# A decoder layer with expert gathers on one Trainium2 core: the prompt's eight tiles in five parts (1, 1, 2, 2, 2) in place of four (2, 2, 2, 2)

## The chip, the core and the metric

The kernel runs on one core of one Trainium2 chip. The metric is the device time of one launch in microseconds. The profile is of one further execution. Engines are named as in the profile: PE (TensorE matmul), PEld (its weight loads), DVE (VectorE), ACT (ScalarE), POOL (GpSimd), SP (SyncE, which issues ordinary DMAs).

## What is computed

One layer for 1024 prompt tokens (eight tiles of 128) and 8 sample tokens, with all numbers in float32:

```python
n1 = rmsnorm(x, norm1_g)
proj = n1 @ w_in                 # q/k/v, GLA q/k/v, output gate, forget gate input, two branch gates
oa = attention over a window of 128 positions, with sinks
og = gated linear attention: a recurrence over the tokens, state (4, 128, 256)
u = sigmoid(ga) * oa + sigmoid(gb) * og
h = x + u @ w_out
x' = h + peer(rmsnorm(h, norm2_g))
```

```python
def peer(...):                    # per token: 8 heads x 16 experts = 128 pairs
    q = xk @ peer_wq
    s = q . subkeys ; top 16 of each half ; top 16 of the 256 sums -> eidx
    g = softmax(sv)
    act = gelu(peer_u[eidx] . xk)             # a row of 1024 numbers for each pair
    return sum(g * act * peer_v[eidx])        # another row of 1024 numbers for each pair
```

So every tile needs 128 gathers of `u` rows and 128 of `v` rows; a gather takes one row of 4 KB for each of the 128 tokens, 512 KB together.

## The kernel before

The prompt is worked in **parts** (`c` in the code; `CH[c]` is the number of tiles in part `c`, `FIRST[c]` its first tile). A part goes through these **stages**, each for all tiles of the part together: norm; `fm` (19 blocks of the feature-major projection, L966); `va`; attention (`at`, L982 to L1007, with the `vb` units); the forget gate (`gate`, L1029); the recurrence (`gla`, L1053 to L1072, four heads); the projections `rb`, `gb` and the branch gate `ga`; the merge (`mg`) and `wo`; the second norm (`n2`); the routing query with the best keys of each half (`q`, L1123, L1130, L1631 to L1642); and `rt`, the choice of the 128 pairs on DVE (`route_tile`), which writes `eidx` at L1539. The eight sample tokens ride along in part `SC` = 2 as a ninth short tile, with stages of their own (`sgla`, `sr`).

All weights come as 38 units of 1 MB (`UNITS`) through `wring`, two buffers deep, and every part loads all 38 again (L738). A unit of `fm` or `wq` has the weights as the stationary operand and the part's tokens as the moving one, so its matmuls are 128 x (128 times the number of tiles). A token-major unit (L926) has one run of eight 128x256 matmuls for each tile.

**Gathers beside the mixer.** The experts of tile t are gathered and used while the next part is computed. The work is cut into **steps** of two pairs (`pool_quad`, `pe_quad`, `act_quad`, `dve_quad`): POOL issues two `u` rows and, 12 pairs later in the order (`LAG`), the `v` rows, through a ring of 12 rows (`ringb`, L662); DVE forms the dot products (L1428); the weighted sum of the `v` rows is formed partly on PE (with a diagonal matrix, L836) and partly on DVE (L1473). Each of the tiles has 64 steps. The first part has no tile before it and runs with no steps at all. In every later part `marks(c)` spreads the steps of the tiles of the part before evenly over the stages: at each point of the program, PE, ACT, DVE and SP first work off all steps up to the mark (`beside`, `quads`). POOL has nothing else to do and is held only by `eidx` and by free ring rows. `MARGIN` = 8 steps are left over at a part's end. `BY_PE` says what share of the `v` rows PE takes in a stage.

The tiles of a part after its first are routed late: the first tile's `eidx` is made at the end of the part, the others' inside the next part's `fm` stage.

```python
def marks(c):
    lo = 0 if c == 1 else SEG_STEP[SEG_OF[FIRST[c - 1]]] - MARGIN
    hi = SEG_STEP[SEG_OF[FIRST[c]]] - MARGIN
```

**The first part's order.** `mixer_order(c)` has two orders: for part 0, if it has two tiles, attention and recurrence are interleaved by hand and the `ga` units stand behind them (`together(c)` is then true); for all others attention comes first, then the gates, then the recurrence with a `ga` unit inside it.

```python
    if c or CH[c] != 2:
        return at + [("between", 0), ("gate", 0), ("gate", 1)] + [x for pair in zip(A, B) for x in pair]
```

**The end.** When the last part is done, its two tiles' experts are left. From `WHOLE` on (the last tile; step 394 = `QW` + 6) the `u` and the `v` row of a pair come as one piece of 8 KB from an array that holds both side by side (L657), into twelve pieces of space that the mixer no longer needs.

Of the kernel before, what the change touches and what calls it, by code (L numbers as in the profile page):

```python
# [8 lines left out]
SEQ = 1024  # L9
NS = 8  # L10
TILES = SEQ // P
CH = (2, 2, 2, 2)
NCH = len(CH)
TM = max(CH)
SC = 2
ST = TM
FIRST = [sum(CH[:c]) for c in range(NCH)]
CM = TM * P
# [35 lines left out]
DIAGS = 4  # L54
XS = FIRST[SC] + CH[SC] - 1
MARGIN = 8
# [108 lines left out]
def tiles_of(c):  # L165

    return [(t, P) for t in range(CH[c])] + ([(ST, NS)] if c == SC else [])


def pair_jobs(c):  # L170

    return [(t, min(2, CH[c] - t), P) for t in range(0, CH[c], 2)] + ([(ST, 1, NS)] if c == SC else [])

# [1873 lines left out]
```

## Time and profile before

| | before |
|---|---|
| median of 3 runs | 3768.2 us (3760.38 to 3772.49) |
| profiled execution, its own time | 3731.8 us |
| its span | 3730.0 us |
| mean granted TensorE clock | 0.871 |
| PE busy | 2881.6 us (77%) |
| DVE busy | 2804.2 us (75%) |
| POOL busy | 2234.3 us (60%) |
| ACT busy | 735.9 us (20%) |
| moved by DMA | 1294.61 MB, mean 347 GB/s |

A part ends, for this text, where the `eidx` of its first tile is written (L1539). These writes stand at 457.4, 1186.5, 2109.9 and 2987.8 us, so the parts take 458, 729, 923 and 878 us, and the end 742 us. A share of busy time is a mean over stretches with different limits; the stretches are read one by one below. In windows, a dot product is two records (the operation and a read of its accumulator), and a float32 matmul is two records as well.

### The profile page before, as it was taken

The numbers are of one execution on the slowest core, as the hardware profiler recorded it, in microseconds if no ns is written. First come the engines' busy times: TensorE is split into PE (matmuls) and PEld (weight loads), VectorE is DVE, ScalarE is ACT, GpSimd is POOL, SyncE is SP. The second block draws the span as 40 slices with busy tenths as digits, with TensorE's granted clock in tenths as the row PEclk, the third lists the DMA queues.
The fourth block names the chain that finished last, engine by engine and source line by source line (L and its number), as shares of the span: only waits on it lengthen the run. The fifth ranks groups of instructions, "written<-read, shape, count | busy, mean of one in ns | idle before, by whom it ended". The sixth has DMA issues, their size and how long they took to land.

```text
span 3730.0 us, 33134 instructions
## 1 busy us (share of the span) xinstructions
PE 2881.6 (77%) x10016; PEld 1798.5 (48%) x10016; DVE 2804.2 (75%) x5740; ACT 735.9 (20%) x1784; POOL 2234.3 (60%) x1820
## 2 busy tenths in 40 slices
PE   8888589788687999788988776978769755655665
PEld 6777566456562666453665344635556311111111
DVE  0641797887788957876879997888788867777776
ACT  1321113322111123223111111422211111111111
POOL 0000076787567656875766777778767776555553
PEclk9899799999898998888999888989879877777677
DMA  4124399999999999989999999999999998999997
GB/s 153 46 87 167 116 405 403 360 358 401 421 391 357 384 354 333 337 318 371 389 396 389 326 389 372 394 353 361 387 421 398 330 392 366 426 426 426 426 426 329
DMA packets 304256, 1294.61 MB, mean 347 GB/s; under 512 B 35288, under 2 KB 44528, under 8 KB 251184
## 3 DMA queue, kind: packets, MB, share of 16 engines
q0 software_dynamic: 260352, 1082.25, 74.2%
q1 hardware_dynamic: 43728, 210.25, 14.5%
q8 instruction: 82, 1.34, 0.1%
q14 instruction: 94, 0.77, 0.1%
HBM read 1276.77 MB, written 17.66 MB: 347 GB/s over the span
## 4 chain that ended last, share of the span: by engine, by line
DMA 26%; PE 23%; POOL 21%; DVE 16%; issue 9%; DVEq 2%; ACT 1%; PEld 1%; PEldq 0%; ACTq 0%; SPq 0%; POOLq 0%
POOL ringb L662 20%; DMA ringb<-in_v,eidx 9%; PE bank L926 8%; DMA ringb<-in_uv,eidx 7%; PE vsum L836 6%; DVE ringb L1428 4%; PE bank L1123 3%; DMA arena<-in_uv,eidx 3%; DMA n2t<-in_uv,eidx 2%; DVE acc L1473 2%; DMA wring<-in_uv,eidx 2%; PE bank L966 2%; DVE scT L1844 1%; DMA ringb<-in_u,eidx 1%; PE bank L982 1%
## 5 line engine op out<-in xcount | busy, mean ns | idle before, releaser
L662 POOL DMA_INDIRECT ringb<-in_u,eidx x768 | 920.3, 1198 | 859.5 <-DVE eidx L1539 455.3
L836 PE MATMUL vsum<-ringb,diag 128*128 128x512 f32 x1908 | 1081.8, 711 | 416.9 <-DMA ringb<-in_v,eidx 261.2
L662 POOL DMA_INDIRECT ringb<-in_v,eidx x768 | 921.6, 1200 | 327.0 <-issue 219.9
L1428 DVE CUSTOM_DVE_ANT_0 ringb<-ringb,n2t 128x1024 f32<-128x1024 f32 x776 | 922.7, 1223 | 118.0 <-DMA ringb<-in_u,eidx 56.2
L836 PEld LDWEIGHTS vsum<-ringb,diag 128*128 128x128 f32 x1908 | 399.8, 223 | 982.3 <-issue 706.1
L926 PE MATMUL bank<-wring,nTb 128*128 128x256 f32 x3024 | 686.7, 388 | 32.6 <-DMA wring<-in_w 29.0
L926 PEld LDWEIGHTS bank<-wring,nTb 128*128 128x128 f32 x3024 | 548.2, 183 | 175.0 <-DMA wring<-in_w 34.4
L1473 DVE SCALAR_TENSOR_TENSOR acc<-ringb,wgt,acc 128x1024 f32<-128x1024 f32 x354 | 454.9, 1285 | 111.7 <-DMA ringb<-in_v,eidx 107.8
L1160 ACT ACTIVATE diag<-cst,wgt 128x128 f32<-128x128 f32 x542 | 209.7, 398 | 962.4 <-DVE wgt L1445 599.3
L966 PE MATMUL bank<-nTb,wring 128*128 128x256 f32 (+1 forms) x1152 | 266.8, 390 | 6.1 <-DMA wring<-in_w 3.1
L657 POOL DMA_INDIRECT ringb<-in_uv,eidx x126 | 178.0, 1412 | 140.7 <-DVE vgb L1473 71.2
L966 PEld LDWEIGHTS bank<-nTb,wring 128*128 128x128 f32 x1152 | 225.9, 196 | 61.6 <-issue 21.3
L1123 PE MATMUL bank<-nTb,wring 128*128 128x256 f32 (+1 forms) x1024 | 234.8, 383 | 1.2 <-ACT nTb L1179 1.2
L1123 PEld LDWEIGHTS bank<-nTb,wring 128*128 128x128 f32 x1024 | 194.9, 192 | 50.2 <-issue 23.6
L1428 DVE CUSTOM_DVE_ANT_0 ringb<-ringb,oab 128x1024 f32<-128x1024 f32 x126 | 154.1, 1225 | 76.0 <-DMA ringb<-in_uv,eidx 76.0
L1179 ACT ACTIVATE arena<-bank 128x256 f32<-128x256 f32 (+1 forms) x160 | 71.5, 467 | 498.4 <-PE bank L1123 277.3
L938 PE MATMUL bank<-cst,oab 128*128 128x128 f32 (+1 forms) x216 | 40.0, 362 | 125.2 <-DVE oab L1676 60.5
L836 PE MATMUL vsum<-wring,diag 128*128 128x512 f32 x88 | 62.3, 847 | 49.9 <-ACT diag L1160 49.9
L938 PEld LDWEIGHTS bank<-cst,oab 128*128 128x128 f32 (+1 forms) x216 | 36.2, 198 | 131.5 <-DVE oab L1676 44.7
L836 PE MATMUL vsum<-nTb,diag 128*128 128x512 f32 x88 | 65.3, 884 | 44.4 <-ACT diag L1160 44.4
L836 PE MATMUL vsum<-qkb,diag 128*128 128x512 f32 x84 | 63.0, 891 | 38.3 <-ACT diag L1160 38.1
L1200 ACT ACTIVATE Pbb<-bank 128x512 f32<-128x512 f32 (+1 forms) x60 | 33.1, 552 | 292.7 <-PE bank L926 292.6
(290 smaller groups left out, 3080.1 us busy)
## 6 DMA issues: line engine op xcount, KB each, us to landing
wring<-in_w SPq DMA_DIRECT2D x152, 1024.0 KB, 7.8
ringb<-in_u,eidx POOLq DMA_INDIRECT x768, 7.3
ringb<-in_v,eidx POOLq DMA_INDIRECT x768, 7.5
n2t<-scratch_n SPq DMA_DIRECT2D x14, 512.0 KB, 7.1
oab<-in_xp SPq DMA_DIRECT2D x4, 1024.0 KB, 6.8
bTb<-in_keysT SPq DMA_DIRECT2D x4, 1024.0 KB, 11.4
vgb<-in_xp SPq DMA_DIRECT2D x4, 1024.0 KB, 8.9
arena<-in_s SPq DMA_DIRECT2D x8, 512.0 KB, 10.2
```

The source lines that it names most:

```text
L657: pool.indirect_dma_start(out=piece[s], out_offset=None, in_=a["uv"], in_offset=place).then_inc(piece_here[s], 16)
L662: pool.indirect_dma_start(out=ring[r], out_offset=None, in_=a["u"] if kind == "u" else a["v"], in_offset=place)\
L836: last = mm(out[:, g * 512:(g + 1) * 512], lhs, row[:, g * 512:(g + 1) * 512], start=(x == first), stop=(x == end))
L926: last = mm(ps[0:R, i * UC:(i + 1) * UC], nT[:, k, lo:lo + R], w[:, k, :], start=(k == 0), stop=(k == KC - 1))
L938: last = tr(ps[:, i * R:(i + 1) * R], oa[0:R, t, k * P:(k + 1) * P], ident[0:R, 0:R])
L966: last = mm(ps[0:M, 0:wide], lhs, nT[:, k, 0:wide], start=(k == 0), stop=(k == KC - 1))
L982: last = mm(ps[:, i * 256:(i + 1) * 256], qaT[lo:lo + 64, 4 * Q + 2 * g + i, t * P:(t + 1) * P], kaT[lo:lo + 64, Q, t * P:(t + 2) * P], st ...
L1123: last = mm(ps[:, 0:wide], w[:, k, (q % 2) * P:(q % 2 + 1) * P], nT[:, k, 0:wide], start=(k == 0), stop=(k == KC - 1))
L1160: A(diag[:, n % DIAGS, :], ident, ACT.Copy, scale=wgt[:, m % 2, at:at + 1]).then_inc(diag_ready, 1)
L1179: A(dst, src, ACT.Copy, scale=scale).then_inc(evac["act"].sem, evac["act"].did(key))
L1428: v.tensor_tensor_reduce(out=row, in0=row, in1=n2, scale=1.0, scalar=0.0, op0=ALU.mult, op1=ALU.add, accum_out=dg[:, m % 2, at:at + 1]).th ...
L1473: STT(y, row, wgt[:, m % 2, at:at + 1], y, ALU.mult, ALU.add).then_inc(used(("v", x))[0], 1)
```

## The change

The table of parts gets five entries. Nothing else is edited.

```diff
-CH = (2, 2, 2, 2)
+CH = (1, 1, 2, 2, 2)
```

All other tables follow from it. The parts begin at tiles 0, 1, 2, 4, 6. Part 0 and part 1 hold one tile each; part 2 (still `SC`) holds tiles 2 and 3 and the sample tokens; the last part is again tiles 6 and 7. The segments of expert work are 0, 1, 2, 3, S, 4, 5, 6, 7 where they were 0, 1, 2, 3, 4, 5, S, 6, 7. The marks of the parts with gathers now run over the steps 0 to 56 (part 1), 56 to 120 (part 2), 120 to 252 (part 3) and 252 to 386 (part 4); they ran over 0 to 120, 120 to 248 and 248 to 386. `QW` stays 388 and `WHOLE` stays 7. Part 0 no longer has two tiles, so `together(0)` is false.

The start of PE's program, before (bank is PSUM, nTb the normalized tokens, wring the weights, kaT and arena keys and queries, Pbb the scores):

```order
L938 MATMUL bank<-cst,oab 128x128 x16
L966 MATMUL bank<-nTb,wring 128x256 x144
L966 MATMUL bank<-nTb,wz 16x256 x8
L926 MATMUL bank<-wring,nTb 128x256 x16
L1029 MATMUL bank<-zbT,wg 128x256 x4
L982 MATMUL bank<-kaT,arena 128x256 x4
L926 MATMUL bank<-wring,nTb 128x256 x16
L982 MATMUL bank<-kaT,arena 128x256 x4
L995 MATMUL bank<-cst,Pbb 128x128 x8
```

and with the change:

```order
L938 MATMUL bank<-cst,oab 128x128 x8
L966 MATMUL bank<-nTb,wring 128x128 x144
L966 MATMUL bank<-nTb,wz 16x128 x8
L926 MATMUL bank<-wring,nTb 128x256 x8
L982 MATMUL bank<-kaT,arena 128x256 x4
L926 MATMUL bank<-wring,nTb 128x256 x8
L982 MATMUL bank<-kaT,arena 128x256 x4
L926 MATMUL bank<-wring,nTb 128x256 x8
L995 MATMUL bank<-cst,Pbb 128x128 x8
```

The same 144 projection matmuls have half the columns, a token-major unit has 8 matmuls in place of 16, and the gate (L1029) has moved behind the attention.

PE in part 2, from the gate to the second head of the recurrence, before (vsum is the weighted sum of `v` rows, two matmuls for each row):

```order
L1029 MATMUL bank<-zbT,wg 128x256 x4
L1034 MATMUL bank<-fmS,wg 128x8 x4
L836 MATMUL vsum<-ringb,diag 128x512 x12
L1053 MATMUL bank<-arena 128x128 x7
L1053 MATMUL bank<-qkb 128x128
L1053 MATMUL bank<-arena 128x128 x7
L1053 MATMUL bank<-qkb 128x128
L1057 MATMUL bank<-cst,arena 128x128 x2
L836 MATMUL vsum<-ringb,diag 128x512 x4
...
L836 MATMUL vsum<-ringb,diag 128x512 x6
L926 MATMUL bank<-wring,nTb 128x256 x16
L926 MATMUL bank<-wring,nTb 8x256 x8
L836 MATMUL vsum<-ringb,diag 128x512 x6
```

and with the change:

```order
L1029 MATMUL bank<-zbT,wg 128x256 x4
L1034 MATMUL bank<-fmS,wg 128x8 x4
L836 MATMUL vsum<-ringb,diag 128x512 x8
L1053 MATMUL bank<-arena 128x128 x7
L1053 MATMUL bank<-qkb 128x128
L1053 MATMUL bank<-arena 128x128 x7
L1053 MATMUL bank<-qkb 128x128
L1057 MATMUL bank<-cst,arena 128x128 x2
L836 MATMUL vsum<-ringb,diag 128x512 x4
...
L836 MATMUL vsum<-ringb,diag 128x512 x2
L926 MATMUL bank<-wring,nTb 128x256 x16
L926 MATMUL bank<-wring,nTb 8x256 x8
L836 MATMUL vsum<-ringb,diag 128x512 x2
```

The part's own matmuls are the same; about half the rows of the gathered experts stand between them.

## Rows read from the trace of the kernel before

**Rows 1.** The page: busy time of the engines over the whole span.
```profile
PE 2881.6 (77%) x10016; PEld 1798.5 (48%) x10016; DVE 2804.2 (75%) x5740; ACT 735.9 (20%) x1784; POOL 2234.3 (60%) x1820
```
**Rows 2.** The page: DMA busy tenths and GB/s in 40 equal slices.
```profile
DMA  4124399999999999989999999999999998999997
GB/s 153 46 87 167 116 405 403 360 358 401 421 391 357 384 354 333 337 318 371 389 396 389 326 389 372 394 353 361 387 421 398 330 392 366 426 426 426 426 426 329
```
**Rows 3.** Windows, one for each part and one for the end.
```profile
core 0: us, PE busy (x) PEld busy (x) DVE busy (x) ACT busy (x) POOL busy (x), PEclk, DMA share, GB/s
0.00:458.00 458.00, 369.04 (x1792) 317.70 (x1792) 192.79 (x582) 92.82 (x209) 2.17 (x13) 0.92 0.31 112
458.00:1187.00 729.00, 595.22 (x2236) 405.16 (x2236) 611.88 (x1244) 166.36 (x367) 529.21 (x446) 0.91 0.99 385
1187.00:2110.00 923.00, 805.06 (x3000) 496.69 (x3000) 728.27 (x1550) 209.25 (x508) 630.19 (x516) 0.90 0.95 360
2110.00:2988.00 878.00, 675.75 (x2372) 440.85 (x2373) 731.00 (x1457) 178.56 (x403) 650.01 (x547) 0.89 0.98 377
2988.00:3730.00 742.00, 436.50 (x618) 138.11 (x616) 540.23 (x910) 88.87 (x297) 422.76 (x301) 0.74 0.97 403
```
**Rows 4.** Waits: who held POOL before its first gather.
```profile
POOL ringb L662 <- DVE eidx L1539: 455.3, 1, 455.3
```
**Rows 5.** Windows of the dot products alone (L1428), parts 1 to 3: DVE busy.
```profile
458.00:1187.00 729.00, 277.04 (x464) 0.91 0.99 385
1187.00:2110.00 923.00, 306.83 (x516) 0.90 0.95 360
2110.00:2988.00 878.00, 327.23 (x548) 0.89 0.98 377
```
**Rows 6.** Windows of part 0: norm, fm, mixer, gates, merge, query, choice.
```profile
0.00:22.00 22.00, 3.65 (x16) 3.27 (x16) 4.46 (x9) 5.16 (x7) 2.11 (x12) 1.00 0.57 217
22.00:90.00 68.00, 67.87 (x305) 57.52 (x305) 0.03 (x1) 6.89 (x18) 0.00 (x0) 1.00 0.38 136
90.00:234.00 144.00, 117.28 (x602) 98.35 (x602) 96.43 (x198) 49.35 (x121) 0.00 (x0) 0.86 0.11 39
234.00:320.00 86.00, 83.92 (x393) 73.65 (x392) 15.52 (x28) 15.76 (x33) 0.00 (x0) 1.00 0.41 147
320.00:361.00 41.00, 33.31 (x160) 28.97 (x160) 5.49 (x8) 7.49 (x13) 0.00 (x0) 0.92 0.59 203
361.00:424.00 63.00, 62.27 (x318) 55.42 (x316) 38.74 (x224) 6.86 (x18) 0.00 (x0) 1.00 0.41 152
424.00:458.00 34.00, 0.75 (x5) 0.52 (x4) 32.11 (x116) 1.29 (x2) 0.06 (x1) 0.57 0.09 31
```
**Rows 7.** Timeline of PE in part 0: runs of 256 and of 128 columns.
```profile
22.13 64.36 PE L966 MATMUL bank<-nTb,wring 128*128 128x256 f32 x288 [0.83 <-DVE nTb L1684]
127.21 1.04 PE L995 MATMUL bank<-cst,Pbb 128*128 128x128 f32 x8
```
**Rows 8.** DMA issues: the weights at 20 to 90 us, and over the span.
```profile
wring<-in_w SPq DMA_DIRECT2D x9, 1024.0 KB, 4.7
...
wring<-in_w SPq DMA_DIRECT2D x152, 1024.0 KB, 7.8
```
**Rows 9.** Timeline of PE: two heads of part 0's recurrence begin.
```profile
197.31 1.80 PE L1053 MATMUL bank<-ringb 128*128 128x128 f32 x14 [1.00 <-issue]
...
221.66 3.33 PE L1053 MATMUL bank<-ringb 128*128 128x128 f32 x14 [8.42 <-issue]
```
**Rows 10.** Windows of part 2: attention, recurrence, sample recurrence with gates.
```profile
1339.00:1505.00 166.00, 152.71 (x686) 101.45 (x684) 117.88 (x222) 50.65 (x138) 98.58 (x85) 0.87 0.90 329
1531.00:1665.00 134.00, 115.10 (x433) 71.97 (x433) 114.34 (x183) 33.84 (x58) 98.99 (x77) 0.88 0.90 327
1665.00:1852.00 187.00, 169.29 (x603) 92.01 (x601) 142.98 (x227) 47.06 (x106) 130.80 (x101) 0.93 0.98 376
```
**Rows 11.** Window of part 2, the sums of `v` rows on PE alone (L836).
```profile
1187.00:2110.00 923.00, 304.16 (x564) 115.78 (x564) 0.90 0.95 360
```

## The prediction

> **What bounds the kernel now.** I read the page first, then the program by parts, then part 0 by stages. Over the whole span no engine is full: PE 77%, DVE 75%, POOL 60% [rows 1]. The slices show two regimes: five slices with DMA at 1 to 4 tenths, then 9 tenths to the end [rows 2]. By parts [rows 3]: part 0 has no gathers, and POOL waits 455.3 us for the first `eidx` [rows 4]; parts 1 to 3 have PE 82, 87 and 77% busy, DVE 84, 79 and 83%, DMA 99, 95 and 98%; the end has DMA at 97% and 403 GB/s.
>
> The question is which of these near-full resources sets the pace of parts 1 to 3. DMA's share says the stream of gathers. But at the same share the rate is 385, 360 and 377 GB/s there and 426 in five slices of the end [rows 2, 3]; in the attention and the recurrence of part 2 it is 329 and 327, with PE at 92 and 86% of these windows [rows 10]. There the mixer's own work, with the steps placed between, sets the pace, and the ring is merely kept full. The Trainium skill (Perfetto Trace Analysis, Identifying the Most-Contended Engine) says to judge DMA by the bandwidth of memory and not by occupancy, since 16 engines make occupancy misleading. By that rule the parts are at 85 to 90% of the 426 that this trace reaches, so not purely bound by DMA.
>
> So I treat a part beside gathers as own work plus a price for each step. The dot products give the steps: 464, 516 and 548 records are 116, 129 and 137 steps [rows 5]. A step costs PE 304.16 / 129 = 2.4 us [rows 11] and DVE 306.83 / 129 = 2.4 us for dots [rows 5] and about 1.2 us for its share of the sums. Between part 0 and part 1, both of two tiles, lie 729 - 458 = 271 us for 116 steps [rows 3]: **2.3 us a step**. The most that a step costs is a whole part over its steps, 729 / 116 = 6.3 us.
>
> **The change, part by part.**
>
> **Part 0, one tile: 458 -> 310.** By the stages of [rows 6]:
> - norm 22 -> 19: the loads stay, one tile's statistics and transposes go.
> - fm 68 -> 41. A 256-column record takes 64.36 / 288 = 223 ns; at 128 columns the eight of L995 give about 115 ns with their tail off [rows 7]. A unit is then 32 x 0.113 = 3.6 us. But a buffer of the ring is reloaded only after use, and a load lands 4.7 us after issue [rows 8]: with two buffers a unit takes (3.6 + 4.7 + 0.4)/2 = 4.35 us. Nine make 39, and 2 for the block of 16 columns. Weights, hidden today, become the pace.
> - mixer 144 -> 110. Halving gives 72, but the chains do not halve and the hand-made overlap is lost. One unit of `va` 4; six steps of attention, four of them with PE work of 2 + 3.5 + 1 + 1.9 = 8.4 us, 39; the gate with its table loads 16, now in nobody's shadow; four heads at 12.5 make 50 (with two tiles a head without much beside it takes 221.66 - 197.31 = 24.4 us [rows 9]).
> - gates 86 -> 38: eight units outside the recurrence in place of twelve, each (3.5 + 4.7 + 0.3)/2 = 4.25 us, and 4 at the ends.
> - merge 41 -> 30, query 63 -> 37 (eight units at 4.65), choice 34 -> 32 (one tile's choice already).
>
> Sum 307, called 310; ends 290 and 345. A page would put fm lower: the Trainium skill (TensorE: Matmul & The Clock Gate, Back-to-back issue gap) gives some 81 ns for a matmul of 128 columns in a stream, which would make a unit (2.6 + 4.7 + 0.4)/2 = 3.85 us and this stage 4 us shorter. The row shows about 113 ns, and the row is used.
>
> **Part 1, one tile beside tile 0: new, 425.** Its marks end at step 56; parts ended some 4 steps before their marks (116 for 120), so 52 steps. Own work 310 - 10 (the first loads) = 300; 52 x 2.3 = 120; and 5 for weights, which land in 7.8 us beside gathers [rows 8], a unit of (3.5 + 7.8)/2 = 5.7 us, mostly filled with steps. Lower end 390, which is what DMA needs: 44 MB at 2.5 us and 200 gathers at 1.4 us. (Parts 1 to 3 hold 446, 516 and 547 gathers, by POOL's counts, and 47, 62 and 44 MB besides, in 722, 877 and 860 us of busy DMA [rows 3]; these two prices fit all three within 3%.) Upper end 470.
>
> **Part 2, two tiles and the sample beside tile 1 alone: 923 -> 745.** This carries the forecast. Its own matmuls stay; 64 steps remain of 129. PE's own work is 805.06 - 304.16 = 501 us [rows 3, 11], DVE's about 270. The 65 steps removed give back a price between 2.4 us (PE's share alone, PE being 87% busy) and 6.3 (all on the path; excluded, since it would leave 514 us, just PE's own busy time with no step in it). I take 2.6, near PE's row: 923 - 169 = 754, and 10 less as only one tile comes before, with none routed late. Ends: 501 + 64 x 2.4 = 655 busy on PE, hence 670; and 825 at 1.5 a step. DMA needs only some 510 us here (256 gathers at 1.4, 62 MB at 2.5): **it idles nearly a third of this part**, and what it fails to move here it cannot move elsewhere.
>
> **Parts 3 and 4: 1607 -> 1680.** They are the old parts 1 and 3 in kind: two tiles beside two tiles. Together they hold 132 + 134 = 266 steps for 253. The 13 more at 5.6 us (2.1 MB at 377 GB/s) are 73 us. The eight loads of the samples' rows, once at the border of the end, now stand in SP's queue among the weights of part 4's fm stage, each held by the use of the row two before it: 0 to 25 us, taken at 0, since the marks pace the weights there too. Ends 1650 and 1720.
>
> **End: 742 -> 742.** It starts at the same step with the same pieces.
>
> **Sum** against the profiled execution: 310 + 425 + 745 + 1680 = 3160 where 458 + 729 + 923 + 878 = 2988 stood: **+172 us**, 3731.8 -> 3904. Its own time is 36 us under the median; on the median I forecast 3768.2 + 172 = **3940 us**. In short: 148 us less at the start buys a second pass of one tile's chains (300) and 100 us of weights (38 MB at 2.5), and a part 2 that can't use the stream.
>
> **The rivals.**
> - **Faster: the stream is the pace everywhere.** If DMA at 95 to 99% means what it says, parts 1 to 4 take the old 2530 us plus 38 MB of weights at 2.5 us, 100, and the stream starts 148 us earlier: 3768 - 148 + 100 = 3720. It decides if part 2 takes under about 570 us with part 1 at 425. For it: the shares. Against it: PE's 655 us of work in part 2 and the 327 GB/s of [rows 10]. Chance 0.08.
> - **All lower ends at once:** 295 + 390 + 670 + 1650 = 3005, +17, 3785: mixer and steps overlap nearly perfectly. Against it: a head's chain of DVE, ACT and PE in turn leaves 8.42 us idle on PE with no step beside it [rows 9]. Chance 0.09, half of it within the bound of no change.
> - **Worse: chains don't shrink.** Part 0 at 345, part 1 at 470, part 2 at 825, parts 3 and 4 at 1690: 3330, +342, 4110. For it: dependent small operations cost nearly as much for one tile as for two. Chance 0.10.
> - **The change does not do what it says:** were the last tiles' pieces or the samples' place to break the order of the end, the end would differ. `QW` and `WHOLE` are the same numbers, so I leave it 0.01, at 3990.
>
> **How the numbers follow.** The forecast has 0.72. Its own range, from half-way ends, is 3850 to 4030. For 8 in 10 it reaches to the rivals on both sides: 3835 to 4050. A difference of about 0.3% is what a measurement of this kernel can tell from none. Faster: 0.08. Same: 0.04. Slower: 0.88.
>
> **What would show it.** First `eidx` at 310 (290 to 345), with PE waiting for `wring` in fm; the second about 425 later; part 2 near 745 with DMA's share at 0.7 to 0.8 and well under 330 GB/s, PE at 85 to 90%; parts 3 and 4 at 6.3 us a step with DMA at 0.95 and more; the end at 742. The forecast is wrong if part 2 keeps DMA above 0.9, or if the first two parts together take under 600 us.

## The result and the profile after

The changed kernel is slower: 3944.39 us median (3919.72 to 3954.34, 4 runs) against 3770.34 us (3760.38 to 3775.82, 4 runs), a ratio of 1.0455 with a 95% interval of 1.0401 to 1.0509. It is +174 us on the medians. The profiled execution took 3940.9 us, with a span of 3939.1.

The profiled executions differ by 209 us, more than the medians, because the one of before lay 39 us under the median of 3770.34 and the one of after 3 us under its own. Single spans compared below carry an uncertainty of that size. So do parts: experiment 4's kernel has the same parts 1 to 3 as the kernel before, and in its profile they took 741, 940 and 897 us where [rows 3] have 729, 923 and 878, some 2% more.

The same views as of before. From the page of the changed kernel, busy time and the DMA slices (answering to [rows 1, 2]):

```profile
PE 2919.1 (74%) x10584; PEld 1843.7 (47%) x10584; DVE 2827.0 (72%) x5840; ACT 766.7 (19%) x1871; POOL 2219.2 (56%) x1820
...
DMA  5358899867677779999999999999999999999997
GB/s 193 108 191 317 325 387 390 307 240 270 209 278 263 283 253 362 381 387 345 357 408 420 356 339 415 374 375 347 351 419 393 370 327 364 426 426 426 426 426 333
```

All engines have nearly the same busy time as before in a longer span. The stream starts in the fourth slice, two slices earlier than in [rows 2], but from the eighth to the fifteenth it runs at 209 to 307 GB/s.

The windows by part, and the dot products alone (two records each, two dots a step), parts 1 to 4, answering to [rows 3, 5]:

```profile
core 0: us, PE busy (x) PEld busy (x) DVE busy (x) ACT busy (x) POOL busy (x), PEclk, DMA share, GB/s
0.00:305.00 305.00, 197.54 (x1180) 174.43 (x1180) 119.93 (x383) 64.87 (x149) 2.11 (x12) 0.89 0.44 159
305.00:729.00 424.00, 316.75 (x1380) 233.64 (x1380) 290.69 (x644) 90.87 (x214) 237.36 (x203) 0.86 0.93 355
729.00:1473.00 744.00, 645.20 (x2717) 433.22 (x2716) 477.44 (x1135) 163.97 (x412) 311.00 (x258) 0.91 0.75 262
1473.00:2322.00 849.00, 651.74 (x2319) 429.78 (x2320) 706.87 (x1422) 178.82 (x397) 622.93 (x512) 0.88 0.97 373
2322.00:3196.00 874.00, 684.33 (x2387) 435.85 (x2386) 684.62 (x1344) 181.19 (x403) 633.60 (x533) 0.89 0.97 375
3196.00:3939.00 743.00, 423.50 (x604) 136.76 (x603) 547.50 (x917) 87.01 (x296) 412.24 (x306) 0.76 0.96 400
```

```profile
305.00:729.00 424.00, 128.76 (x216) 0.86 0.93 355
729.00:1473.00 744.00, 152.46 (x256) 0.91 0.75 262
1473.00:2322.00 849.00, 310.41 (x520) 0.88 0.97 373
2322.00:3196.00 874.00, 318.60 (x532) 0.89 0.97 375
```

| part | before | steps | after | steps | forecast |
|---|---|---|---|---|---|
| 0 | 458 | 0 | 305 | 0 | 310 |
| 1, one tile | | | 424 | 54 | 425 |
| 2, with the samples | 923 | 129 | 744 | 64 | 745 |
| the two others of two tiles | 729 + 878 | 253 | 849 + 874 | 263 | 1680 |
| end | 742 | 134 | 743 | 135 | 742 |

Part 2 has PE at 645.20 / 744 = 87% and DMA at 75%. Its attention, its recurrence and its sample recurrence with gates, answering to [rows 10]:

```profile
838.00:965.00 127.00, 121.97 (x638) 88.60 (x636) 73.18 (x159) 38.34 (x117) 48.07 (x44) 0.92 0.70 242
990.00:1099.00 109.00, 91.35 (x380) 62.31 (x381) 85.71 (x139) 25.74 (x42) 47.30 (x37) 0.89 0.62 209
1099.00:1264.00 165.00, 152.03 (x571) 86.00 (x570) 93.29 (x158) 37.79 (x91) 66.69 (x52) 0.93 0.77 273
```

The three take 127, 109 and 165 us where [rows 10] have 166, 134 and 187: with half the steps they lose 12 to 23%, and the rate of DMA falls with them. The stages of part 0 (norm, fm, mixer, gates, merge, query, choice), answering to [rows 6]:

```profile
0.00:19.00 19.00, 1.94 (x8) 1.57 (x8) 2.44 (x6) 4.01 (x5) 2.11 (x12) 1.00 0.59 224
19.00:62.00 43.00, 38.52 (x304) 36.97 (x304) 0.01 (x1) 4.99 (x18) 0.00 (x0) 1.00 0.58 199
62.00:165.00 103.00, 71.15 (x361) 60.04 (x360) 55.16 (x144) 35.66 (x80) 0.00 (x0) 0.85 0.26 91
165.00:205.00 40.00, 31.87 (x143) 26.26 (x141) 7.64 (x19) 9.47 (x22) 0.00 (x0) 1.00 0.64 236
205.00:234.00 29.00, 17.68 (x80) 14.33 (x80) 3.41 (x7) 4.74 (x8) 0.00 (x0) 0.93 0.70 249
234.00:275.00 41.00, 36.39 (x288) 35.25 (x288) 22.86 (x117) 5.42 (x18) 0.00 (x0) 0.93 0.58 210
275.00:305.00 30.00, 0.00 (x0) 0.00 (x0) 28.41 (x93) 0.58 (x1) 0.00 (x0) 0.54 0.09 34
```

### The profile page after: what moved, and what is told of

Same layout as the page of the kernel before. It is cut to its first block, busy times and chain, and to the rows that moved or that the text cites. A ratio compares the mean times of both kernels' runs of the same rounds, so it can differ in the third digit from the quotient of the medians.

```text
span 3939.1 us, 34706 instructions
## 1 busy us (share of the span) xinstructions
PE 2919.1 (74%) x10584; PEld 1843.7 (47%) x10584; DVE 2827.0 (72%) x5840; ACT 766.7 (19%) x1871; POOL 2219.2 (56%) x1820
## 4 chain that ended last, share of the span: by engine, by line
PE 26%; DMA 25%; DVE 20%; POOL 14%; issue 10%; DVEq 2%; ACT 1%; another core or an unknown queue 1%; ACTq 1%; SPq 0%; PEldq 0%; PEld 0%; POOLq 0%
POOL ringb L662 13%; PE bank L926 10%; DMA ringb<-in_uv,eidx 7%; PE vsum L836 5%; DVE ringb L1428 5%; DMA ringb<-in_v,eidx 5%; DMA wring<-in_w 4%; DVE acc L1473 3%; PE bank L966 3%; DMA arena<-in_uv,eidx 3%; PE bank L1123 2%; DMA n2t<-in_uv,eidx 2%; DMA wring<-in_uv,eidx 2%; PE bank L982 1%; PE bank L1053 1%
## 5 line engine op out<-in xcount | busy, mean ns | idle before, releaser
L662 POOL DMA_INDIRECT ringb<-in_u,eidx x768 | 945.9, 1232 | 986.7 <-DVE dg L1428 479.7
L836 PE MATMUL vsum<-ringb,diag 128*128 128x512 f32 x1908 | 1083.3, 710 | 472.1 <-DMA ringb<-in_v,eidx 278.8
L662 POOL DMA_INDIRECT ringb<-in_v,eidx x768 | 897.1, 1168 | 423.6 <-issue 218.5
L1428 DVE CUSTOM_DVE_ANT_0 ringb<-ringb,n2t 128x1024 f32<-128x1024 f32 x776 | 923.7, 1223 | 148.9 <-DMA ringb<-in_u,eidx 69.1
L836 PEld LDWEIGHTS vsum<-ringb,diag 128*128 128x128 f32 x1908 | 398.7, 223 | 1021.7 <-issue 725.6
L926 PE MATMUL bank<-wring,nTb 128*128 128x256 f32 x3024 | 701.7, 391 | 62.8 <-DMA wring<-in_w 54.7
L966 PE MATMUL bank<-nTb,wring 128*128 128x128 f32 (+2 forms) x1440 | 283.4, 359 | 28.4 <-DMA wring<-in_w 25.5
L966 PEld LDWEIGHTS bank<-nTb,wring 128*128 128x128 f32 x1440 | 248.2, 208 | 79.8 <-DMA wring<-in_w 28.2
L1123 PE MATMUL bank<-nTb,wring 128*128 128x128 f32 (+2 forms) x1280 | 247.8, 349 | 11.9 <-DMA wring<-in_w 9.9
L1123 PEld LDWEIGHTS bank<-nTb,wring 128*128 128x128 f32 x1280 | 214.5, 200 | 59.8 <-issue 25.0
L1428 DVE CUSTOM_DVE_ANT_0 ringb<-ringb,oab 128x1024 f32<-128x1024 f32 x126 | 154.3, 1226 | 77.7 <-DMA ringb<-in_uv,eidx 77.7
L1179 ACT ACTIVATE arena<-bank 128x256 f32<-128x256 f32 (+2 forms) x184 | 76.0, 429 | 553.9 <-PE bank L1123 232.3
L1721 DVE SCALAR_TENSOR_TENSOR Pbb<-cst,bank 128x256 f32<-128x256 f32 x128 | 46.9, 415 | 128.7 <-PE bank L982 126.0
L1053 PE MATMUL bank<-arena 128*128 128x128 f32 x448 | 73.6, 331 | 62.8 <-DVE arena L1832 42.9
L1631 DVE MAX8 val<-bank 128x8 f32<-128x128 f32 (+1 forms) x144 | 36.7, 288 | 99.2 <-PE bank L1130 74.9
L1053 PEld LDWEIGHTS bank<-arena 128*128 128x128 f32 x448 | 69.5, 242 | 75.5 <-DVE arena L1832 51.9
```

Source lines behind the costliest of these rows:

```text
L662: pool.indirect_dma_start(out=ring[r], out_offset=None, in_=a["u"] if kind == "u" else a["v"], in_offset=place)\
L836: last = mm(out[:, g * 512:(g + 1) * 512], lhs, row[:, g * 512:(g + 1) * 512], start=(x == first), stop=(x == end))
L926: last = mm(ps[0:R, i * UC:(i + 1) * UC], nT[:, k, lo:lo + R], w[:, k, :], start=(k == 0), stop=(k == KC - 1))
L966: last = mm(ps[0:M, 0:wide], lhs, nT[:, k, 0:wide], start=(k == 0), stop=(k == KC - 1))
L1053: last = mm(ps[:, i * P:(i + 1) * P], kk, qq, start=True, stop=True)
L1123: last = mm(ps[:, 0:wide], w[:, k, (q % 2) * P:(q % 2 + 1) * P], nT[:, k, 0:wide], start=(k == 0), stop=(k == KC - 1))
```

## The experiments

Every number "in part n" below is from that run's profile, between the writes of `eidx`; ratios are to runs of the kernel before in the same comparison. The kernel before took 3728 to 3770 us at the median from comparison to comparison, so absolute times of different comparisons are 1% uncertain against each other.

**1. Does a step cost its time or a share of a saturated stream? Steps before the own work.** The marks of part 2 (then of part 1) are raised, so that most of the part's steps run first and its own work after them nearly alone:

```diff
         done += w
+    if c == 2:                     # e8: c == 1
+        out = {k: max(v, hi - 10) for k, v in out.items()}
     return out
```

> The changed kernel with the marks of part 2 raised to at least step 110: 54 of its 64 steps run before the part's own work, which then runs nearly alone. Theory (own work plus 2.6 us a step): 54 steps alone at 5.2 to 5.7 us (280 to 310), then 570 to 610 for the own work with ten steps; part 2 takes 860 to 910 in place of 744. Rival (the gathers stretched the mixer, or the mixer the gathers): own work under 500 us, part 2 at 790 or less.

> The changed kernel with the marks of part 1 raised to at least step 46: 46 of its steps run before the one-tile part's own work, which then runs nearly alone. Theory (the second pass over one tile costs about what part 0 cost, some 295 us without the first loads): 46 steps alone, twelve of them with u rows only, in 210 to 230 us, then 300 to 320 us for the own work with its last steps; part 1 takes 510 to 550 in place of 424. Rival (much of part 1's 424 us is the gathers, the own work is nearer 210, half of a two-tile part): own work under 250, part 1 under 480.

Windows of e5 (the steps alone, then part 2's own work), and its dot products in the same two:

```profile
732.00:1024.00 292.00, 158.56 (x216) 50.04 (x216) 208.22 (x296) 32.26 (x77) 225.51 (x219) 0.75 1.00 397
1024.00:1659.00 635.00, 541.97 (x2504) 393.45 (x2504) 273.84 (x839) 128.18 (x331) 46.45 (x40) 0.91 0.36 126
```
```profile
732.00:1024.00 292.00, 137.07 (x224) 0.75 1.00 397
1024.00:1659.00 635.00, 19.02 (x32) 0.91 0.36 126
```

Windows of e8, the same two stretches of part 1:

```profile
311.00:548.00 237.00, 111.25 (x136) 34.27 (x136) 156.81 (x229) 18.14 (x46) 186.90 (x165) 0.62 0.97 359
548.00:870.00 322.00, 239.58 (x1243) 195.49 (x1244) 139.09 (x412) 68.17 (x163) 47.24 (x38) 0.87 0.56 201
```

Part 2 took 927 us and part 1 560 us, both longer than expected (860 to 910, and 510 to 550). The own work can be read off: 635 us for part 2 with eight steps in it, and 322 us for part 1 with eight steps. Taking off 2 us for each step, an estimate, leaves 619 and 306 us. Each kernel ran once, so these two numbers have no interval. Alone, 56 steps take 292 us, 5.2 us each, with DMA at 1.00. The rivals (own work under 500 and under 250 us) fall. So interleaving is worth much: beside the mixer a step of part 2 costs (744 - 619) / 64 = 2.0 us and one of part 1 (424 - 306) / 54 = 2.2 us, not 5.2. (What the weights lose by landing more slowly beside gathers is in this price.) The own work of part 2 came out some 40 us above the 579 us that 745 - 64 x 2.6 implied, and the price of a step below 2.6; the two errors cancel in the sum. Between 64 and 129 steps the price is (923 - 744) / 65 = 2.75, or (940 - 744) / 65 = 3.0 with the part 2 of experiment 4's profile. Some of that is the late routing of a tile, which only the longer part contains; the prediction gave it 10 us, and no run separates it. Parts of two tiles without samples say the same: 470 us without a step (experiment 4), 545 with 54 steps (experiment 6), 729 with 116 [rows 3], so 1.4 us for each of the first 54 and 3.0 for each of the next 62. **The price rises with the density of the steps.**

**2. Is the stream of transfers the pace?** The changed kernel with 38 more copies of 1 MB, memory to memory, one beside each weight unit of one part:

```diff
                     sp.dma_start(wring[:, n % WR, :, :]..., a["w"][i]).then_inc(d_w[n % WR], 16)
+                    if c == 2:                     # e3: c == 3
+                        sp.dma_start(o["extra"][i], a["w"][i]).then_inc(d_extra, 16)
```

> The changed kernel plus 38 copies of 1 MB from memory to memory on SP's queue, one beside each weight unit of part 2 (the one beside tile 1's gathers alone). Theory (DMA is not the pace there, some 27% of it idle): part 2 goes from 744 to 750 to 775, DMA share to 0.9 or more, +5 to +30 us in all (3950 to 3975). Rival (the stream of transfers is the pace everywhere): +95 us in part 2 (4040).

> The same 38 copies in part 3, which runs beside two tiles' gathers. Theory (there DMA at 0.97 is close to the pace): 849 goes to 920 to 950, +70 to +100 us (4015 to 4045). Rival (mixer and steps set the pace in every part, DMA's share is only a full ring): under +30 us (3975 or less).

Windows of e2 (part 2) and of e3 (part 3):

```profile
737.00:1482.00 745.00, 641.21 (x2717) 430.13 (x2716) 476.99 (x1135) 163.80 (x412) 311.24 (x258) 0.91 0.84 313
```
```profile
1484.00:2393.00 909.00, 668.87 (x2321) 435.58 (x2322) 707.87 (x1420) 178.44 (x397) 612.08 (x511) 0.85 0.99 390
```

In part 2 the copies cost nothing: 745 us for 744, while DMA's share rose from 0.75 to 0.84 (0.9 or more was expected). The whole kernel took 3957.94 us (1.0525, interval 1.0483 to 1.0567, which overlaps that of the change). Its profile is 18 us longer than the changed kernel's, and these lie in part 0 (313 us) and part 4 (884), where nothing was added, not in part 2. In part 3 they cost 909 - 849 = 60 us, 1.6 us per MB, less than the 70 to 100 expected. The kernel took 4005.76 us in all (1.0624, 1.0578 to 1.0670), 48 us more than e2, which moves the same bytes and ran in the same comparison. The copies stand in the same places of SP's queue in both, so the queue isn't what costs the time. Both extremes fall: the stream is not the pace everywhere, and it is not just a full ring where its share is 0.97.

**3. Do the weights set the pace of one-tile units?** In parts 0 and 1 only the first half of each weight unit is loaded after the first two; the other half of the buffer keeps what it held, so the projections use partly old weights.

```diff
+                    if c < 2 and n >= WR:
+                        sp.dma_start(wring[:, n % WR, 0:KC // 2, :]..., a["w"][i][:, 0:KC * UC // 2])...
```

> The changed kernel, with only the first half of each weight unit loaded in parts 0 and 1 (after the first two units); the other half of the buffer keeps what it held. Theory (weights reload is the pace of the one-tile units): part 0 from 305 to about 287, part 1 from 424 to about 404, -38 us in all (3905). Rival (chains of dependent operations are the pace, the loads are covered): within 8 us of no change in both parts.

Timeline of PE in part 0's fm, the changed kernel and then e4 (start, us, operation, what ended the idle time before it; 64 records are two units):

```profile
19.07 10.16 PE L966 MATMUL bank<-nTb,wring 128*128 128x128 f32 x64 [0.78 <-DVE nTb L1684]
30.52 7.52 PE L966 MATMUL bank<-nTb,wring 128*128 128x128 f32 x64 [1.29 <-DMA wring<-in_w]
39.17 7.59 PE L966 MATMUL bank<-nTb,wring 128*128 128x128 f32 x64 [1.13 <-DMA wring<-in_w]
```
```profile
19.26 10.02 PE L969 MATMUL bank<-nTb,wring 128*128 128x128 f32 x64 [0.79 <-DVE nTb L1687]
29.56 7.41 PE L969 MATMUL bank<-nTb,wring 128*128 128x128 f32 x64 [0.29 <-DMA wring<-in_w]
37.45 7.41 PE L969 MATMUL bank<-nTb,wring 128*128 128x128 f32 x64 [0.47 <-DMA wring<-in_w]
```

The reload shows as predicted: two units in 8.65 us (30.52 to 39.17) in place of 7.5 of pure work, and 7.9 with half loads. Part 0 fell from 305 to 295 us, part 1 from 424 to 404, and the kernel to 3913.94 us (1.0378, 1.0335 to 1.0422), about -30 us where -38 was expected (the two intervals just overlap). Part 1 is right at -20; part 0 gave 10 of 18 against this trace, and 16 against the 311 and 313 us that e3 and e2 had in the same comparison.

**4. The hand-made order.** The kernel before, with part 0 in the plain order:

```diff
-    if c or CH[c] != 2:
+    if True:
```

> Four parts of two tiles as before, but part 0 in the plain order (attention, gates, recurrence with the ga units inside). Theory (own work plus a price per step; part 0 lost a hand-made overlap when it got one tile): the first eidx comes at about 480 us in place of 457, everything later is unchanged, +20 us in all (3790). Rival (the order is worth nothing, the chain of dependent operations is the same): first eidx at 455 to 462, no change.

3787.86 us, ratio 1.0070 (1.0047 to 1.0092). The window of part 0 is 23 us longer than in [rows 3], and PE's busy time is the same within 2 us: only overlap was lost.

```profile
0.00:480.00 480.00, 370.93 (x1792) 320.62 (x1792) 193.83 (x579) 98.10 (x213) 2.11 (x12) 0.90 0.30 107
```

It also gives the own work of a plain two-tile part, 480 us, or 470 without the first loads. A one-tile part has 306. **Half the tokens cost 65% of the time.**

The stages tell where the rest comes from. Without the norm, the changed part 0 takes 286 us, 57 more than half of the plain part's 458. By [rows 6], with the 23 us of the order counted to the mixer and the gates, that is 9 in fm and 9 or 10 in the query, 16 or 17 in mixer and gates, 8 or 9 in the merge, and 13 in the choice, which is one tile's work in both. Reloading is a part of it: PE waits 7.0 us for weights in the gates' window (165 to 205 us) and 4.0 in the query's. The chains of the recurrence do shrink almost with the tile: the last two heads of the changed part 0 begin 13.3 us apart, where [rows 9] have 24.4.

```profile
144.96 1.80 PE L1053 MATMUL bank<-arena 128*128 128x128 f32 x14 [1.95 <-ACTq L1203]
158.28 1.80 PE L1053 MATMUL bank<-arena 128*128 128x128 f32 x14 [1.79 <-ACTq L1203]
```

**5. Can the idle DMA of part 2 be bought back?** 26 steps of tile 0 move from part 1 into part 2:

```diff
-    lo = 0 if c == 1 else SEG_STEP[SEG_OF[FIRST[c - 1]]] - MARGIN
-    hi = SEG_STEP[SEG_OF[FIRST[c]]] - MARGIN
+    lo = 0 if c == 1 else SEG_STEP[SEG_OF[FIRST[c - 1]]] - (34 if c == 2 else MARGIN)
+    hi = SEG_STEP[SEG_OF[FIRST[c]]] - (34 if c == 1 else MARGIN)
```

> The changed kernel with the border between the marks of parts 1 and 2 at step 30 in place of 56: 26 steps move from part 1 into part 2, where DMA idles. Theory (a step costs its time on PE and DVE wherever it stands): part 1 from 424 to about 364, part 2 from 744 to about 812, sum within 15 us of no change (3930 to 3960), DMA share in part 2 to 0.9. Rival (idle DMA in part 2 is the loss): steps moved there are nearly free, part 2 stays under 765, -40 us in all (3905).

> The changed kernel itself again, on the chip of the next run. Theory: 1.040 to 1.051 times the kernel before.

> 26 steps moved from part 1 into part 2 again, beside the changed kernel on one chip. Theory (a step costs nearly the same in both parts): within 10 us of the changed kernel, or up to 25 us faster, since the run before had parts 1 and 2 at 1146 us together against 1168. Rival (idle DMA is the whole loss): 40 us faster or more.

The first run (e7) gave 1.0485 (1.0451 to 1.0518), with parts 1 and 2 at 358 and 788 us; the comparison held no run of the changed kernel. In the next one the changed kernel had 1.0462 (1.0425 to 1.0499), and the moved steps 1.0464 (1.0444 to 1.0484). Parts 1 and 2 of e9 and of e10:

```profile
309.00:730.00 421.00, 312.09 (x1380) 229.89 (x1380) 290.77 (x643) 90.75 (x214) 236.29 (x202) 0.86 0.93 357
730.00:1469.00 739.00, 639.45 (x2717) 428.93 (x2716) 477.56 (x1137) 163.99 (x412) 310.52 (x258) 0.92 0.75 264
```
```profile
314.00:679.00 365.00, 250.53 (x1252) 203.01 (x1252) 207.50 (x520) 77.24 (x177) 120.12 (x102) 0.83 0.72 267
679.00:1484.00 805.00, 695.86 (x2820) 452.74 (x2820) 562.22 (x1259) 179.44 (x447) 421.31 (x354) 0.91 0.85 306
```

421 + 739 = 1160 us against 365 + 805 = 1170, and the medians are 3944.5 and 3947.89 us. The steps that moved (24 or 25 by the dot products) were not free in part 2: it took 66 us more, and part 1 56 less. The rival falls. What moved with them was the idle DMA, from part 2 into part 1. Both parts together hold the same steps in either kernel, so this shows that the idle DMA of part 2 isn't there for the taking; it doesn't show what more steps in the two parts together would cost, since no further tile's `eidx` exists yet.

**6. Another division.**

```diff
-CH = (2, 2, 2, 2)
+CH = (1, 2, 2, 2, 1)
```

> Parts of 1, 2, 2, 2, 1 tiles. Theory (a part takes the longer of own work plus 2.3 to 2.6 us a step, and what DMA needs, about 6.2 us a step with its weights): 305 + 590 + 923 + 870 + 820 and 390 for the end of one tile, a span near 3900, median 3930; the last part of one tile is held by DMA. Rival (purely own work plus a price per step, 2.3): that part takes 606 us, span 3685, faster than before by 45 us.

3843.97 us, ratio 1.0303 (1.0267 to 1.0338): faster than the change, slower than before. Its parts are 314, 545, 910, 842 and 815 us and 408 for the end, a span of 3834. The forecast of a span near 3900 was 66 us too high (on a median of 3768 for the kernel before the ratio gives 3882, where 3930 stood). Part 1 (two tiles beside one) and part 4 (one tile beside two):

```profile
314.00:859.00 545.00, 463.71 (x1988) 354.52 (x1988) 364.97 (x840) 124.27 (x277) 237.59 (x202) 0.92 0.77 279
...
2611.00:3426.00 815.00, 531.34 (x1762) 303.01 (x1763) 617.41 (x1150) 143.42 (x334) 614.21 (x533) 0.82 1.01 401
```

The one-tile part beside two tiles took 815 us, within 5 of the 820 forecast from DMA's needs. The price of 2.3 us per step alone would have given 606. DMA is the bound there, as its share of 1.01 at 401 GB/s and PE at 65% say. Most of the miss is part 1, forecast 45 us too high, and part 3 (28 too high). In part 1, with 54 steps over two tiles, a step costs (545 - 470) / 54 = 1.4 us.

**7. The samples' loads in SP's queue.** The timeline of SP in the changed kernel, in part 4's fm stage:

```profile
2368.19 0.33 SPq L690 DMA_DIRECT2D n2t<-scratch_n  x1
2375.39 0.33 SPq L738 DMA_DIRECT2D wring<-in_w  x1
2375.81 23.17 SPq L690 DMA_DIRECT2D n2t<-scratch_n  x6
2399.03 0.42 SPq L738 DMA_DIRECT2D wring<-in_w  x1
```

Six loads of sample rows, each held by a used buffer, keep SP for 23 us, and the next weights are issued only then. The edit puts them behind the last part's weights. It also moves four steps from part 3 into part 4 (the mark between them falls from 252 to 248), so only the sum of the two parts can be compared:

```diff
-XS = FIRST[SC] + CH[SC] - 1
+XS = 5
```

> The changed kernel with the samples' segment behind tile 5, as in the kernel before (XS = 5), so that its eight loads of n2 rows stand behind the last part's weights and not among those of its fm stage. Theory (SP is held there for 23 us by loads that wait for their buffers, and the weights of fm behind it come late): parts 3 and 4 together from 1724 to about 1700, -20 to -30 us in all, 1.039 to 1.041 times the kernel before. Rival (the loads are hidden): no change beyond 8 us.

> The changed kernel itself beside the run before, on its chip. Both theories: 1.044 to 1.048 times the kernel before.

e11 has 3905.98 us, 1.0475 (1.0457 to 1.0494), and the control 3913.92 us, 1.0491 (1.0473 to 1.0509). The control lies just above its expected 1.044 to 1.048. The difference is 8 us with overlapping intervals, the rival's bound. Parts 3 and 4 of e11, and of the control:

```profile
1468.00:2289.00 821.00, 638.72 (x2308) 424.95 (x2309) 693.91 (x1403) 175.28 (x391) 593.62 (x497) 0.89 0.97 376
2289.00:3157.00 868.00, 674.36 (x2382) 440.16 (x2381) 702.37 (x1367) 183.98 (x409) 649.66 (x549) 0.90 0.98 383
```
```profile
1481.00:2320.00 839.00, 645.53 (x2320) 426.71 (x2321) 707.45 (x1422) 178.44 (x397) 617.99 (x512) 0.89 0.98 378
2320.00:3183.00 863.00, 676.73 (x2387) 436.99 (x2387) 684.67 (x1343) 180.51 (x403) 633.80 (x533) 0.89 0.98 380
```

1689 us against 1702. My expectation of -20 to -30 falls: the stall of 23 us in SP's queue is worth 8 us by the medians and 13 by the profiles, and neither is clear of noise. The trace of the changed kernel shows why it could not be worth much. In part 4's norm and fm, 2322 to 2480 us, PE waits for no weights at all. Its largest wait there is for `v` rows (11 times, 27.6 us together), and over the same stages e11 has 27.8 us of it:

```profile
PE vsum L836 <- DMA ringb<-in_v,eidx: 27.6, 11, 8.5
```

## Why the prediction was right, point by point

- **Part 0 (310; measured 305).** Every stage came within 7 us of its term. Fm took 43 for 41; its units are reload-bound, as e4 shows (8.65 us for two, forecast 8.7). The mixer took 103 for 110, the gates 40 for 38, merge 29 for 30, query 41 for 37, choice 30 for 32. The lost hand-made order was counted among the mixer's terms; e1 prices it at 23 us for two tiles. The stage sum held, though the 305 us are the shortest of this part: e2, e3, e5 and e7 to e12 have 308 to 315.
- **Part 1 (425; measured 424).** Shown by e8: 306 us of own work where 300 was assumed, and 2.2 us a step for 2.3.
- **Part 2 (745; measured 744).** The size is right, the split is not. Own work is about 619 us and not 579 (e5), and a step costs 2.0 us at 64 steps, below PE's own 2.4. The own matmuls fill 645.20 - 149.12 = 496 of the 619 us, which leaves room for a part of the steps. What the forecast rests on is the price of the *removed* steps: 169 us for 65 of them and 10 for the late routing, 179 together, and 923 - 744 = 179 was measured. Against e1's part 2 it is 196, so the match to 1 us is partly luck. That DMA has slack here is shown by e2, where 38 MB more cost nothing; its share was 0.75, within the forecast 0.7 to 0.8, though the sum of prices had it idle for nearly a third.
- **Parts 3 and 4 (1680; measured 1723).** This term was 43 us too low. There are ten more steps than before, not 13: the forecast set the marks of after (266) against the counts of before (253). All 263 took 6.55 us each, where [rows 3, 5] gave 6.35. Part of it is the quick execution from which the price was taken, 36 us under its median: e1, whose parts 1 and 3 have the same steps as before, took 741 and 897 us, 6.47 us a step, and 263 steps at that price are 1702. Two more profiles of the changed kernel have 1731 (e9) and 1702 (e12), the second in a comparison where the kernel before took only 3728 us. So 20 to 30 us are left over the steps at either level. The samples' loads, priced 0 to 25 and taken at 0, may be 8 to 13 of them (e11, not clear of noise); the cause of the rest stays open.
- **The end (742; measured 743).** As forecast.
- **The sum.** +172 us was forecast. The medians show +174; the two profiled executions show +209, and the 37 us between are the 43 us of parts 3 and 4 less 6 us in the first parts. So the nearness of 3940 to 3944.39 is better than the working: the missing term and the quick execution of before cancel.
- **The rivals.** "The stream is the pace everywhere" falls by e2, e5 and part 2's 744 us (it needed 570). "All lower ends" and "chains don't shrink" fall by the parts' own times. The weighing of DMA's share against its bandwidth was incomplete: it took as full the 426 GB/s of the end's 8 KB pieces, but the steps alone in e5 run at a share of 1.00 with 397 GB/s, and part 4 of e6 at 1.01 with 401. Against some 400, the 385 and 377 GB/s of the old parts 1 and 3 are 94 to 96%. Where the share is 0.97 to 1.01, more transfers do cost time (e3, e6).

One sentence of the kernel's description above is wrong: `WHOLE` = 7 and step 394 are the segment of tile 6, so both tiles of the last part, and not the last tile alone, come in pieces of 8 KB, before and after. No number of the prediction rests on it.

The cause, then: the change starts the stream 153 us earlier and pays with a second pass over one tile's chains, 306 us of own work where a tile joined to another costs about 470 - 306 = 164. The own work of all parts outside the end grows by 2 x 306 + 10 - 480 = 142 us in the plain order, plus 23 for the lost order, which is 165 of the 174 us.

The steps as a whole cost the same in both, which the profiles of the change and of e1 show. With 306, 619 and 470 us of own work taken off the parts, the 381 steps of the changed kernel cost 118 + 125 + 379 + 404 = 1026 us, and the 382 of e1 cost 271 + 321 + 427 = 1019. That is the net of two shifts: the thinly spread steps of parts 1 and 2 cost 78 us less than e1's part 2 (118 steps for 129), and parts 3 and 4 cost 85 more than e1's parts 1 and 3, for ten more steps. So against e1 the change should cost 142 us, and the ratios 1.0455 and 1.0070 lie 145 us apart. That a part in mid-stream has the 470 us of e1's part 0 as own work was not measured, but it drops out here, since both kernels have two such parts.

Of the 38 MB more of weights, the half that e4 leaves out of part 1 costs 20 us there; what the other half costs, no run shows.

No division that was run beats the kernel before. Parts of three tiles, which would lower the number of passes, were not run.

## What to carry to other kernels

When a first part without overlap is halved to start a stream sooner, compare the time gained at the start with the whole cost of one more pass: measure the own work of the small part (here 65% of the large one's, not half). Stages held by the reload of two buffers and work that is done for one tile in either case don't shrink with the part. Then ask of each part beside the stream which of the two is longer, own work with its steps or the transfers, and take the price of a step from that regime: here 1.4 to 2.2 us with slack, about 3 for each step added between half and full density, 5.2 for steps that run alone with DMA full. A part that DMA holds is better taken whole, with its weights: 6.1 to 6.6 us for each of its steps. Idle DMA in a part is no gain waiting to be taken if moving transfers into it moves their consumers' work too.

## What the runs showed of the hardware that was not expected

- 38 MB of copies from memory to memory, added in a part with DMA at 0.75, raised its share to 0.84 and cost no time (745 us for 744), and in a part at 0.97 cost 60 us, 1.6 us per MB, less than the 2.5 us of the prediction's estimate for weights.
- The kernel before took 3770, 3768, 3734, 3769 and 3728 us at the median in five comparisons, 1% apart. The third and the fourth were on the same chip, 24 minutes apart, so it is not only a matter of the chip. The ratios of one kernel, the changed one, were 1.0455, 1.0462 and 1.0491 with overlapping intervals, so a difference of 0.3% has to be read beside a control in the same comparison.
- A 23 us hold of the issuing queue in front of weight loads was worth 8 us by the medians and 13 by the profiles, not clear of noise, and PE waited for no weights behind it.
